# Seven block products in place of eight for two feed-forward steps

## The chip, the cores and the metric

The kernel runs on one core of one Trainium2 chip. The metric is the device time of one launch in microseconds (us), lower is better. Every time below is from that core.

## The reference

Two layers, each of a feed-forward block, a mixer of three attention branches, and a second feed-forward block, over 256 tokens with 1024 features. The change touches the feed-forward blocks alone; there are four in the run:

```python
D_MODEL = 1024
SEQ = 256
DEPTH = 2
D_FF = 2816

def _swiglu(x, w_gate, w_up, w_down):
    return (jax.nn.silu(x @ w_gate) * (x @ w_up)) @ w_down
...
    for l in range(DEPTH):
        x = x + 0.5 * _swiglu(_rmsnorm(x, ffn1_norm[l]), ffn1_w_gate[l], ffn1_w_up[l], ffn1_w_down[l])
...
        x = x + 0.5 * _swiglu(_rmsnorm(x, ffn2_norm[l]), ffn2_w_gate[l], ffn2_w_up[l], ffn2_w_down[l])
    return _rmsnorm(x, final_norm)
```

## The kernel before

**Three passes.** Every float32 operand is split in two float32r parts, a rounded one (`_hi`) and the rest (`_lo`), and every product is three matmuls: hi by hi, hi by the weights' lo, lo by the weights' hi (`three`, lines 1393 to 1395). The normalised and turned input stands in `ht_hi`, `ht_lo` (1024 features in 8 blocks `k` of 128 rows, 256 tokens in 2 tiles `t` of 128).

**The ring of slabs.** Weights come as slabs of 128 x 2048 float32 (1 MB) through a ring of three slots: `raw`, `whi`, `wlo`. SP loads a slab with two DMAs of 512 KB as soon as its slot's `raw` has been read (it waits for `lo_done` of the slab three before); ScalarE rounds it into `whi` (`convert`, L1138); VectorE subtracts and writes the rest into `wlo` (`convert`, L547); both wait until TensorE has used the slab three before (`slab_used`).

**A step.** A feed-forward block runs in 11 steps (`NSTEP`) of 256 hidden columns (`FSTEP`). Step i has two slabs of gate and up weights (4 blocks k each, 256 gate columns beside 256 up columns) and one slab of down weights. `gate_up(i)` is 2 slabs x 4 blocks x 2 tiles x 3 passes = 48 matmuls of 512 columns into PSUM banks 0 and 1 (tile t in bank t); `down(i)` is 24 matmuls into banks 4 to 7, which gather the block's output over all steps. TensorE's order is gate_up(i), down(i-1), gate_up(i+1), down(i), so the product of step i has one down and one gate_up in which to get ready.

**Between them.** After gate_up(i), ScalarE computes silu of the gate half into `sg` (L1178, one instruction for each tile), VectorE multiplies it with the up half and the row's scale (`products`, L599), and then turns the 256 x 256 product: 16 transposes of 32 partitions each (`turn_product`, L609), which put each 32 x 32 block at its final place. ScalarE rounds the turned product into `at_hi` (`act_round`, L1186), VectorE writes the rest into `at_lo` (`act_rest`, L615). The last two steps use other buffers and the last gate_up uses banks 2 and 3, so that TensorE runs gate_up(9), gate_up(10), down(8), down(9), down(10) at the end. After down(10) VectorE adds the result to `x` (`residual`, L588) and the next block's input is turned by TensorE (`prep`, L1412), rounded by ScalarE, and the rest written by VectorE (L571).

**What sets the order.** Each engine's program is written out by hand in a block of its own, and runs in order; all synchronisation is by counted semaphores. GpSimd (POOL) has nothing to do in a feed-forward block but the row scales; in the mixer it issues DMAs that move 32 x 32 blocks between partitions (`cross`, L1103), the method that the change brings to the feed-forward steps.

## Time and profile before

| | |
|---|---|
| median of 3 runs | 1160.47 us (1158.66 to 1160.72) |
| profiled execution | 1159.99 us, its span 1158.2 us |
| TensorE busy | 1148.3 us, 99% of the span, 5525 matmuls |
| VectorE busy | 935.0 us, 81% |
| ScalarE busy | 581.5 us, 50% |
| GpSimd busy | 73.5 us, 6% |
| DMA | 186 GB/s mean |
| granted TensorE clock | 0.998 |

The span is the time from the first to the last instruction of the profiled execution; the device time has a little more around it. A busy share near 100% on one engine says that it sets the time as long as nothing makes it wait.

### The profile page before, as it was taken

Reading aid. Unit: us, or ns where it says so; the run is one execution under the profiler, and the core shown is the slowest. Engines: PE = TensorE matmul, PEld = TensorE weight load, DVE = VectorE, ACT = ScalarE, POOL = GpSimd, SP = SyncE. Lnnn points to the kernel's source line nnn. Section 1 sums busy time; section 2 is a strip of 40 time slices with the busy share of each in tenths; the row PEclk is TensorE's granted clock in tenths of the full one; section 3 lists DMA queues with packets and bytes.
Section 4 is the critical chain, followed back from the end, with each engine's and each line's share of the span. In section 5 each row is a group of like instructions: output and inputs, shape, how many; then the busy total and the mean of one; then the engine's idle time right before and its main releaser. Section 6 shows DMA issues by size and latency. Waiting matters only on the chain.

```text
span 1158.2 us, 16246 instructions
## 1 busy us (share of the span) xinstructions
PE 1148.3 (99%) x5525; PEld 940.3 (81%) x5525; DVE 935.0 (81%) x1734; ACT 581.5 (50%) x757; POOL 73.5 (6%) x133
## 2 busy tenths in 40 slices
PE   9999999999999999999999999999999999999997
PEld 6888888887777888888888888888877788888886
DVE  6877887878977688778887887877898696888877
ACT  6444345456764464344454444454678635434433
POOL 2000000061000000000000000002510000000000
PEclk9999999999999999999999999999999999999999
DMA  8566555796325555655556556557943345655570
GB/s 289 189 214 216 179 187 163 238 252 199 135 74 182 182 161 202 217 192 183 195 177 202 180 178 218 182 183 216 281 155 108 144 142 182 219 181 168 197 236 37
DMA packets 151042, 215.21 MB, mean 186 GB/s; under 512 B 9184, under 2 KB 110160, under 8 KB 150992
## 3 DMA queue, kind: packets, MB, share of 16 engines
q1 hardware_dynamic: 148256, 209.64, 55.2%
q0 software_dynamic: 2048, 4.20, 1.6%
q10 hardware_dynamic: 688, 0.71, 0.2%
q8 instruction: 30, 0.49, 0.2%
q14 instruction: 20, 0.16, 0.0%
HBM read 209.28 MB, written 1.05 MB: 182 GB/s over the span
## 4 chain that ended last, share of the span: by engine, by line
PE 96%; DMA 2%; DVE 1%; issue 0%; SPq 0%; ACT 0%; POOLq 0%; POOL 0%; DVEq 0%
PE ps L1393 30%; PE ps L1395 29%; PE ps L1394 29%; PE ps L1607 2%; PE ps L1663 1%; PE ps L1635 1%; PE ps L1443 1%; DMA raw<-in_w_in_dram 1%; PE ps L1412 1%; DMA x<-in_x_dram 1%; DVE wlo L547 0%; PE ps L1694 0%; PE ps L1654 0%; SPq L508 0%; PE ps L1578 0%
## 5 line engine op out<-in xcount | busy, mean ns | idle before, releaser
L547 DVE TENSOR_TENSOR wlo<-raw,whi 128x2048 fp32r<-128x2048 f32 (+1 forms) x195 | 433.7, 2242 | 79.8 <-ACT whi L1138 57.7
L1138 ACT ACTIVATE whi<-raw 128x2048 fp32r<-128x2048 f32 (+1 forms) x195 | 366.1, 1879 | 257.6 <-PE ps L1395 251.7
L1393 PE MATMUL ps<-whi,ht_hi 128*128 128x512 f32 (+1 forms) x1192 | 465.5, 391 | 0.6 <-DVE wlo L547 0.6
L1395 PE MATMUL ps<-whi,ht_lo 128*128 128x512 f32 (+1 forms) x1192 | 460.8, 387 | 0.0
L1394 PE MATMUL ps<-wlo,ht_hi 128*128 128x512 f32 (+1 forms) x1192 | 460.3, 386 | 0.0
L1395 PEld LDWEIGHTS ps<-whi,ht_lo 128*128 128x128 f32 x1192 | 223.9, 188 | 46.0
L1393 PEld LDWEIGHTS ps<-whi,ht_hi 128*128 128x128 f32 x1192 | 224.0, 188 | 45.6 <-ACT whi L1138 1.1
L1394 PEld LDWEIGHTS ps<-wlo,ht_hi 128*128 128x128 f32 x1192 | 224.1, 188 | 43.7
L609 DVE STREAM_TRANSPOSE scr<-scr 32x128 f32<-32x128 f32 x688 | 208.4, 303 | 10.3
L1393 PE MATMUL ps<-whi,at_hi 128*128 128x512 f32 x304 | 118.5, 390 | 0.0
L1394 PE MATMUL ps<-wlo,at_hi 128*128 128x512 f32 x304 | 118.3, 389 | 0.0
L1395 PE MATMUL ps<-whi,at_lo 128*128 128x512 f32 x304 | 118.3, 389 | 0.0
L1178 ACT ACTIVATE scr<-ps,rstd 128x256 f32<-128x256 f32 x88 | 37.0, 472 | 130.2 <-PE ps L1395 129.7
L599 DVE SCALAR_TENSOR_TENSOR scr<-ps,rstd,scr 128x256 f32<-128x256 f32 x88 | 38.5, 479 | 55.8 <-ACT scr L1178 55.8
L1393 PEld LDWEIGHTS ps<-whi,at_hi 128*128 128x128 f32 x304 | 57.0, 188 | 12.5 <-issue 0.8
L1395 PEld LDWEIGHTS ps<-whi,at_lo 128*128 128x128 f32 x304 | 57.1, 188 | 11.9
L1394 PEld LDWEIGHTS ps<-wlo,at_hi 128*128 128x128 f32 x304 | 57.1, 188 | 11.8
L1272 ACT ACTIVATE prob<-prob,nmax 128x128 f32<-128x128 f32 (+1 forms) x96 | 42.4, 447 | 6.3 <-DVE nmax L768 6.1
L1089 POOL TENSOR_SCALAR msq<-ssq 128x2 f32<-128x2 f32 x6 | 1.2, 193 | 656.6 <-ACT p_t L1151 656.6
L1166 ACT ACTIVATE ht_hi<-ps,cols 128x256 fp32r<-128x256 f32 x47 | 19.2, 473 | 29.8 <-PE ps L1412 29.8
L1117 POOL TENSOR_SCALAR gates<-gates 128x512 f32<-128x512 f32 x24 | 21.7, 920 | 173.8 <-ACT gates L1244 173.8
L1237 ACT ACTIVATE proj<-ps,rstd 128x512 f32<-128x512 f32 (+1 forms) x24 | 14.2, 644 | 32.9 <-PE ps L1395 32.9
(179 smaller groups left out, 787.4 us busy)
## 6 DMA issues: line engine op xcount, KB each, us to landing
raw<-in_ffn_w_down_dram SPq DMA_DIRECT2D x88, 512.0 KB, 4.8
raw<-in_w_in_dram SPq DMA_DIRECT2D x88, 512.0 KB, 4.6
raw<-in_ffn_w_gate_dram SPq DMA_DIRECT2D x85, 512.0 KB, 4.0
raw<-in_ffn_w_up_dram SPq DMA_DIRECT2D x85, 512.0 KB, 5.0
raw<-in_w_out_dram SPq DMA_DIRECT2D x16, 512.0 KB, 4.5
raw<-in_w_branch_c_dram SPq DMA_DIRECT2D x8, 512.0 KB, 4.2
qk<-gates POOLq DMA_DIRECT2D x32, 64.0 KB, 2.9
gates<-prob POOLq DMA_DIRECT2D x32, 64.0 KB, 6.3
```

The costliest lines, as they stand in the source:

```text
L547: nc.vector.tensor_tensor(wlo[:, n, 0:w], raw[:, n, 0:w], whi[:, n, 0:w].bitcast(F32), ALU.subtract).then_inc(lo_done, 1)
L599: nc.vector.scalar_tensor_tensor(act[:, t, :], ps[:, bank, FSTEP:2 * FSTEP], rstd[:, t:t + 1], sg[:, t, :], ALU.mult, ALU.mult).then_inc(a ...
L609: ins = nc.vector.transpose(dst[q:q + 32, :, :, a:a + 32], src[a:a + 32, :, :, q:q + 32])
L1117: nc.gpsimd.tensor_scalar(gv, gv, 0.5, 0.5, ALU.mult, ALU.add).then_inc(gate_ready, 1)
L1138: nc.scalar.activation(whi[:, n, 0:w], raw[:, n, 0:w], ACT.Copy).then_inc(hi_done, 1)
L1166: nc.scalar.activation(ht_hi[:, k, :], src, ACT.Copy, scale=gain(l, n, k)).then_inc(hth, 1)
L1178: nc.scalar.activation(sg[:, t, :], ps[:, t + step_bank(f, i), 0:FSTEP], ACT.Silu, scale=rstd[:, t:t + 1]).then_inc(silu_done, 1)
L1272: ins = nc.scalar.activation(pv, pv, ACT.Exp, scale=-1.0, bias=nmax[:, b, 4 * t + h:4 * t + h + 1], accum_out=den[:, b, 4 * t + h:4 * t + ...
L1393: nc.tensor.matmul(o, xh, wh, start=start, stop=False)
L1394: nc.tensor.matmul(o, xh, wl, start=False, stop=False)
L1395: return nc.tensor.matmul(o, xl, wh, start=False, stop=stop)
L1607: ins = nc.tensor.matmul(score_head(t, h), queries(row, qb + h // 2, t), keys(row, pair, kb, h // 2, t + 1), start=opens, stop=n >= 6, ski ...
```

## The change

**Seven products for eight.** Steps 8 and 9 (`PAIR` = 8 and the one after) become one (`gate_up_pair`). Their gate and up weights are four blocks of 512 rows x 512 columns, B11 (gate, rows 0 to 511), B12 (up, same rows), B21 and B22 (rows 512 to 1023); the input gives four blocks of 128 tokens x 512 features. Eight block products of 12 matmuls become seven by Strassen's scheme (in Winograd's form), whose inputs are blocks and sums of blocks and whose outputs are added up afterwards.

**Sums of the weights.** The four blocks are loaded once more, whole, into `sum_raw` (8 DMAs of 512 KB spread over steps 2 to 5, `load_part`); VectorE forms four differences (`block_sum`, steps 4 to 6), ScalarE rounds them (`sum_round`, steps 5 to 7), VectorE writes the rests (`sum_rest`, steps 6, 7 and in the pair). B11 (as two half slabs), B21 and B22 also come through the ring.

**Sums of the input** (the standing side of the matmuls): ten additions of 128 x 512 (`side_sums`, five each in steps 1 and 2), four roundings and four rests in step 3.

**Outputs.** The first product is copied from its bank by ScalarE, so is the second; the others are added onto banks by the matmuls themselves or by VectorE (`pair_sums`, `pair_products`). Silu and products of the pair are on 128 x 512.

**Turning by blocks and DMA.** In all steps but the first, VectorE turns the product with 2 transposes of 128 partitions, which leave each 32 x 32 block turned in its own partitions; 16 DMAs of 16 KB, 11 issued by GpSimd and 5 by ScalarE (`cross_act`), move the blocks to their places in `act_blocks` (or, for the last two products, in `T3`'s raw buffer), and `act_round` waits for them. The step loops of VectorE, ScalarE and SP are written out; silu waits for `act_done` and no longer for `atl`.

```diff
+        m1_out = scr[:, 0:512]
+        m5_out, u2, v57, up_1 = (sum_raw["T1"][:, 512 * n:512 * n + 512] for n in range(4))
+        up_0, gate_1 = v57, m5_out
+        sg_2, act_2 = (gated_all[:, 1024 * n:1024 * n + 1024].rearrange("p (t c) -> p t c", t=NT) for n in range(2))
+
+        act_turns = [(v[:, 0:512], v[:, 512:1024]) for v in
+                     (act_blocks, sum_raw["T3"][:, 0:1024], sum_raw["T3"][:, 1024:2048])]
...
+        BY_ACT = [(3, 0), (3, 1), (3, 2), (3, 3), (2, 3)]
+        BY_POOL = [(a, q) for a in range(4) for q in range(4) if (a, q) not in BY_ACT]
...
+        def cross_act(eng, l, f, i, blocks, done):
+
+            eng.wait_ge(act_turned, (l * 2 + f) * NSTEP + i)
+            apart(eng)
+            for a, q in blocks:
+                blocks_in, blocks_out = act_set(i)
+                eng.dma_start(blocks_out[32 * q:32 * q + 32, P * a:P * a + P],
+                              blocks_in[32 * a:32 * a + 32, P * q:P * q + P]).then_inc(done[n_set(i)], 16)
...
-                for a in range(0, P, 32):
-                    for q in range(0, P, 32):
-                        ins = nc.vector.transpose(dst[q:q + 32, :, :, a:a + 32], src[a:a + 32, :, :, q:q + 32])
...
+                    for t in range(NT):
+                        ins = nc.vector.transpose(dst[:, t], src[:, t, :].rearrange("p (j q c) -> p q j c", j=2, q=4))
...
+                o, a, b, parts = ((b11, b12, b11, (0, 1)), (b12, b22, b12, (2,)), (b22, b22, b11, ()),
+                                  (b21, b21, b22, (3,)))[m]
...
+            def pair_sums(l, f):
+
+                r = l * 2 + f
+                dve.wait_ge(pair_out, r * 2 + 2)
+                dve.wait_ge(pair_ps, r * 4 + 2)
+                nc.vector.tensor_tensor(v57, ps[:, 0, :], m5_out, ALU.add).then_inc(pair_sum, 1)
+                dve.wait_ge(pair_ps, r * 4 + 3)
+                nc.vector.tensor_tensor(u2, ps[:, 3, :], m1_out, ALU.add).then_inc(pair_sum, 1)
+                dve.wait_ge(pair_sum, r * 5 + 2)
+                nc.vector.tensor_tensor(up_1, v57, u2, ALU.add).then_inc(pair_sum, 1)
+
+            def pair_products(l, f):
+
+                r, s0 = l * 2 + f, f * (FFN_SLABS + MIX_SLABS)
+                dve.wait_ge(pair_sum, r * 5 + 3)
+                wait_used(dve, l, s0 + PAIR_SLAB + 3)
+                nc.vector.tensor_tensor(up_0, ps[:, 2, :], u2, ALU.add).then_inc(pair_sum, 1)
+                dve.wait_ge(pair_sum, r * 5 + 4)
+                dve.wait_ge(silu_done, r * (2 * NSTEP) + PAIR * 2 + 2)
+                nc.vector.scalar_tensor_tensor(act_2[:, 0, :], up_0, rstd[:, 0:1], sg_2[:, 0, :], ALU.mult,
+                                               ALU.mult).then_inc(act_done, 2)
+                dve.wait_ge(pair_ps, r * 4 + 4)
+                nc.vector.tensor_tensor(gate_1, ps[:, 0, :], u2, ALU.add).then_inc(pair_sum, 1)
+                dve.wait_ge(silu_done, r * (2 * NSTEP) + PAIR * 2 + 4)
+                nc.vector.scalar_tensor_tensor(act_2[:, 1, :], up_1, rstd[:, 1:2], sg_2[:, 1, :], ALU.mult,
+                                               ALU.mult).then_inc(act_done, 2)
...
-                with dve.Fori(1, last - 1) as i:
-                    convert(l, (i, s0 + 2))
+                for i in range(1, PAIR):
+                    w = SLAB // 2 if i == PAIR - 1 else SLAB
+                    convert(l, s0 + 3 * i + 2, w)
                     products(l, f, i)
                     turn_product(l, f, i)
-                    convert(l, (i, s0 + 3))
-                    convert(l, (i, s0 + 4))
-                    act_rest(l, f, i)
-                convert(l, s0 + 3 * last - 1)
-                products(l, f, last - 1)
-                turn_product(l, f, last - 1)
-                convert(l, s0 + 3 * last)
-                act_rest(l, f, last - 1)
-                convert(l, s0 + 3 * last + 1)
+                    convert(l, s0 + 3 * i + 3, w)
+                    if i < PAIR - 1:
+                        convert(l, s0 + 3 * i + 4)
+                    if i < 3:
+                        side_sums(l, f, i - 1)
+                    if i == 3:
+                        for m in range(4):
+                            side_rest(l, f, m)
+                    for m in {4: (0,), 5: (1, 2), 6: (3,)}.get(i, ()):
+                        block_sum(l, f, m)
+                    for m in {6: (0,), 7: (1, 2)}.get(i, ()):
+                        sum_rest(l, f, m)
+                    if i < PAIR - 1:
+                        act_rest(l, f, i)
+                for m in range(2, 5):
+                    convert(l, s0 + PAIR_SLAB + m)
+                act_rest(l, f, PAIR - 1)
+                pair_sums(l, f)
+                sum_rest(l, f, 3)
+                convert(l, s0 + PAIR_SLAB + 5)
+                pair_products(l, f)
+                turn_product(l, f, PAIR)
+                turn_product(l, f, PAIR + 1)
+                convert(l, s0 + OUT_SLAB)
+                convert(l, s0 + OUT_SLAB + 1)
                 products(l, f, last)
                 turn_product(l, f, last)
-                convert(l, s0 + 3 * last + 2)
+                act_rest(l, f, PAIR)
+                convert(l, s0 + OUT_SLAB + 2)
+                act_rest(l, f, PAIR + 1)
+                convert(l, s0 + OUT_SLAB + 3)
                 act_rest(l, f, last)
                 if not ends(l, f):
-                    convert(l, s0 + 3 * last + 3)
+                    convert(l, s0 + FFN_SLABS)
...
+            def ffn(l, f):
+                norm(l * 3 + 2 * f)
+                with pool.Fori(1, PAIR) as i:
+                    cross_act(pool, l, f, i, BY_POOL, act_crossed_rest)
+                for i in range(PAIR, NSTEP):
+                    cross_act(pool, l, f, i, BY_POOL, act_crossed_rest)
+
...
-                        eng.wait_ge(atl, r * NSTEP + i)
+                        eng.wait_ge(act_done, r * (2 * NSTEP) + i * 2)
...
-                with eng.Fori(1, last - 1) as i:
-                    convert(l, (i, s0 + 2))
+                for i in range(1, PAIR):
+                    w = SLAB // 2 if i == PAIR - 1 else SLAB
+                    convert(l, s0 + 3 * i + 2, w)
                     silu(l, f, i, False)
-                    convert(l, (i, s0 + 3))
-                    convert(l, (i, s0 + 4))
-                    act_round(l, f, i)
-                convert(l, s0 + 3 * last - 1)
-                silu(l, f, last - 1, False)
-                convert(l, s0 + 3 * last)
-                act_round(l, f, last - 1)
-                convert(l, s0 + 3 * last + 1)
+                    convert(l, s0 + 3 * i + 3, w)
+                    cross_act(eng, l, f, i, BY_ACT, act_crossed)
+                    if i < PAIR - 1:
+                        convert(l, s0 + 3 * i + 4)
+                    if i == 3:
+                        side_round(l, f)
+                    for m in {5: (0,), 6: (1, 2), 7: (3,)}.get(i, ()):
+                        sum_round(l, f, m)
+                    if i < PAIR - 1:
+                        act_round(l, f, i)
+                convert(l, s0 + PAIR_SLAB + 2)
+                wait_used(eng, l, s0 + PAIR_SLAB + 1)
+                nc.scalar.activation(m1_out, ps[:, 1, :], ACT.Copy).then_inc(pair_out, 1)
+                convert(l, s0 + PAIR_SLAB + 3)
+                eng.wait_ge(pair_ps, (l * 2 + f) * 4 + 1)
+                nc.scalar.activation(m5_out, ps[:, 2, :], ACT.Copy).then_inc(pair_out, 1)
+                convert(l, s0 + PAIR_SLAB + 4)
+                act_round(l, f, PAIR - 1)
+                convert(l, s0 + PAIR_SLAB + 5)
+                wait_used(eng, l, s0 + PAIR_SLAB + 2)
+                pair_silu(l, f, 0, ps[:, 1, :])
+                convert(l, s0 + OUT_SLAB)
+                eng.wait_ge(pair_sum, (l * 2 + f) * 5 + 5)
+                pair_silu(l, f, 1, gate_1)
+                cross_act(eng, l, f, PAIR, BY_ACT, act_crossed)
+                convert(l, s0 + OUT_SLAB + 1)
+                cross_act(eng, l, f, PAIR + 1, BY_ACT, act_crossed)
                 silu(l, f, last, False)
-                convert(l, s0 + 3 * last + 2)
+                act_round(l, f, PAIR)
+                convert(l, s0 + OUT_SLAB + 2)
+                cross_act(eng, l, f, last, BY_ACT, act_crossed)
+                act_round(l, f, PAIR + 1)
+                convert(l, s0 + OUT_SLAB + 3)
...
+                pe.wait_ge(act_done, r * (2 * NSTEP) + PAIR * 2)
+                for h in range(2):
+                    product(1, quadrant(halves, 0, 0), from_ring(s0 + PAIR_SLAB + h, 2), True, 2 * h)\
+                        .then_inc(slab_used, 1)
+                pe.wait_ge(side_l, r * 4 + 4)
+                product(2, s1, from_sums("T1"), True).then_inc(pair_ps, 1)
+                product(0, s3, from_sums("T3"), True).then_inc(pair_ps, 1)
+                product(3, s2, from_sums("T2"), True).then_inc(pair_ps, 1)
+                pe.wait_ge(pair_out, r * 2 + 2)
+                product(1, quadrant(halves, 0, 1), from_ring(s0 + PAIR_SLAB + 2, 4), False).then_inc(slab_used, 1)
+                product(2, s4, from_ring(s0 + PAIR_SLAB + 3, 4), False).then_inc(slab_used, 1)
+                pe.wait_ge(pair_sum, r * 5 + 1)
+                product(0, quadrant(halves, 1, 1), from_sums("T4"), False).then_inc(pair_ps, 1)
...
-                with pe.Fori(2, last - 1) as i:
+                with pe.Fori(2, PAIR) as i:
                     gate_up(l, f, i)
                     down(l, f, i - 1, (i, s0 + 1))
-                gate_up(l, f, last - 1)
+                gate_up_pair(l, f)
                 gate_up(l, f, last)
-                down(l, f, last - 2, s0 + 3 * last)
-                down(l, f, last - 1, s0 + 3 * last + 1)
+                for n in range(3):
+                    down(l, f, PAIR - 1 + n, s0 + OUT_SLAB + n)
...
+                for i in range(i0, PAIR):
+                    if i == 2:
+                        sp.wait_ge(x_new, (l * 3 + 2 * f) * 4 + 4)
+                        sp.wait_ge(ssq_done, (l * 3 + 2 * f) * NT + NT)
                     for a in range(2):
-                        load_gate_up(l, (i, s0 - 1 + a), wg, wu, a, i * FSTEP)
-                    load_halves(l, (i, s0 + 1), wd, i * FSTEP - FSTEP, 2, 0, D)
-                for i in (last - 1, last):
-                    for a in range(2):
-                        load_gate_up(l, gate_slab(f, i) - 1 + a, wg, wu, a, i * FSTEP)
-                for i in (last - 2, last - 1):
-                    load_halves(l, s0 + 2 * last + 2 + i, wd, i * FSTEP, 2, 0, D)
+                        load_gate_up(l, s0 + 3 * i - 1 + a, wg, wu, a, i * FSTEP)
+                        if i >= 2 and a:
+                            load_part()
+                    load_halves(l, s0 + 3 * i + 1, wd, i * FSTEP - FSTEP, 2, 0, D)
+                    if i >= 2:
+                        load_part()
+                assert not parts
```

What stands in GpSimd's program between the two row-scale groups at the start of a layer; before, nothing (the three rows of each):

```order
L1089 TENSOR_SCALAR msq<-ssq 128x2 [waits x_in2,x_in0,x_in1,ssq_done]
L1091 TENSOR_TENSOR rstd<-msq,mhalf 128x2 [waits rstd_ready]
L1094 TENSOR_SCALAR hrstd<-rstd 128x2 [waits rstd_ready]
L1089 TENSOR_SCALAR msq<-ssq 128x2 [waits ssq_done]
L1091 TENSOR_TENSOR rstd<-msq,mhalf 128x2 [waits rstd_ready]
L1094 TENSOR_SCALAR hrstd<-rstd 128x2 [waits rstd_ready]
```

and now, where `act_blocks` holds the turned product and the loop of the middle rows runs over steps 1 to 7:

```order
L1283 TENSOR_SCALAR hrstd<-rstd 128x2 [waits rstd_ready]
L1296 UNCONDITIONAL_BRANCH
L534 DMA act_blocks<-act_blocks 32x128 [waits act_turned]
L534 DMA act_blocks<-act_blocks 32x128 x10
L1296 REGISTER_ALU
L1296 COMPARE_AND_BRANCH
L534 DMA act_blocks<-act_blocks 32x128 [waits act_turned]
L534 DMA act_blocks<-act_blocks 32x128 x10
L534 DMA T_raw<-T_raw 32x128 [waits act_turned]
```

Eleven DMA issues for each of ten steps have come between the two groups, each wave behind a wait for that step's transposes.

VectorE at the end of a block before, from step 9's products on (`wlo` is a slab's rest, `ht_lo` the last product's, `x` the residual; the transposes are L609):

```order
L599 SCALAR_TENSOR_TENSOR scr<-ps,rstd,scr 128x256 [waits silu_done] x2
L609 STREAM_TRANSPOSE scr<-scr 32x2x2x32 [waits act_done]
L609 STREAM_TRANSPOSE scr<-scr 32x2x2x32 x15
L547 TENSOR_TENSOR wlo<-raw,whi 128x2048 [waits slab_used,hi_done,raw_in2]
L615 TENSOR_TENSOR ht_lo<-scr,ht_hi 128x512 [waits ath]
L547 TENSOR_TENSOR wlo<-raw,whi 128x2048 [waits slab_used,hi_done,raw_in0]
L588 SCALAR_TENSOR_TENSOR x<-ps,x 128x512 [waits sub_out] x2
```

and now, the pair, from the third slab of it on (`T_lo` is the rest of a weight sum, `T_raw<-ps` the sums of banks):

```order
L637 TENSOR_TENSOR wlo<-raw,whi 128x2048 [waits slab_used,hi_done,raw_in2]
L637 TENSOR_TENSOR wlo<-raw,whi 128x2048 [waits slab_used,hi_done,raw_in0]
L713 TENSOR_TENSOR at_lo<-act_blocks,at_hi 128x512 [waits ath]
L764 TENSOR_TENSOR T_raw<-ps,T_raw 128x512 [waits pair_ps,pair_out]
L766 TENSOR_TENSOR T_raw<-ps,scr 128x512 [waits pair_ps]
L768 TENSOR_TENSOR T_raw<-T_raw 128x512 [waits pair_sum]
L756 TENSOR_TENSOR T_lo<-T_raw,T_hi 128x2048 [waits sum_h]
L637 TENSOR_TENSOR wlo<-raw,whi 128x2048 [waits slab_used,hi_done,raw_in1]
L775 TENSOR_TENSOR T_raw<-ps,T_raw 128x512 [waits slab_used,pair_sum]
L778 SCALAR_TENSOR_TENSOR gated_T<-T_raw,rstd,gated_T 128x512 [waits silu_done,pair_sum]
L781 TENSOR_TENSOR T_raw<-ps,T_raw 128x512 [waits pair_ps]
L783 SCALAR_TENSOR_TENSOR gated_T<-T_raw,rstd,gated_T 128x512 [waits silu_done]
```

Between the rests of slabs stand now the output sums, each behind a product of TensorE, and one rest of a weight sum.

## Rows read from the trace of the kernel before

**Rows 1.** The page's head and busy time, share of span and count by engine.

```profile
span 1158.2 us, 16246 instructions
...
PE 1148.3 (99%) x5525; PEld 940.3 (81%) x5525; DVE 935.0 (81%) x1734; ACT 581.5 (50%) x757; POOL 73.5 (6%) x133
```

**Rows 2.** Waits of TensorE: total us, times, longest.

```profile
PE ps L1786 <- DVE scr L986: 1.3, 1, 1.3
...
PE ps L1393 <- DVE wlo L547: 0.6, 2, 0.3
```

**Rows 3.** Timeline of TensorE, step's first down and next gate_up matmul: start, us, work.

```profile
128.32 0.39 PE L1393 MATMUL ps<-whi,at_hi 128*128 128x512 f32 x1
...
133.76 0.39 PE L1393 MATMUL ps<-whi,ht_hi 128*128 128x512 f32 x1
```

**Rows 4.** Timeline of VectorE through that step.

```profile
129.03 0.88 DVE L599 SCALAR_TENSOR_TENSOR scr<-ps,rstd,scr 128x256 f32<-128x256 f32 x2 [1.71 <-ACT scr L1178]
129.95 5.05 DVE L609 STREAM_TRANSPOSE scr<-scr 32x128 f32<-32x128 f32 x16
135.03 4.49 DVE L547 TENSOR_TENSOR wlo<-raw,whi 128x2048 fp32r<-128x2048 f32 x2
139.44 0.69 DVE L615 TENSOR_TENSOR at_lo<-scr,at_hi 128x512 fp32r<-128x512 f32 x1
141.35 2.29 DVE L547 TENSOR_TENSOR wlo<-raw,whi 128x2048 fp32r<-128x2048 f32 x1 [1.23 <-ACT whi L1138]
```

**Rows 5.** Timeline of ScalarE through that step.

```profile
128.53 0.84 ACT L1178 ACTIVATE scr<-ps,rstd 128x256 f32<-128x256 f32 x2 [3.52 <-PE ps L1395]
129.26 1.91 ACT L1138 ACTIVATE whi<-raw 128x2048 fp32r<-128x2048 f32 x1
133.97 1.92 ACT L1138 ACTIVATE whi<-raw 128x2048 fp32r<-128x2048 f32 x1 [2.79 <-PE ps L1395]
135.79 0.61 ACT L1186 ACTIVATE at_hi<-scr 128x512 fp32r<-128x512 f32 x1
139.41 1.92 ACT L1138 ACTIVATE whi<-raw 128x2048 fp32r<-128x2048 f32 x1 [3.00 <-PE ps L1395]
```

**Rows 6.** Groups by line and shape: busy us, mean ns, idle before.

```profile
L558 DVE TENSOR_TENSOR wlo<-raw,whi 128x1024 fp32r<-128x1024 f32 x3 | 3.6, 1223 | 1.8 <-ACT whi L1146 1.8
...
L707 DVE STREAM_TRANSPOSE prob<-gates 128x256 f32<-128x256 f32 x8 | 3.0, 414 | 0.0
```

**Rows 7.** Timeline of GpSimd in the mixer, and one ScalarE DMA issue.

```profile
231.26 9.42 POOL L1103 DMA_DIRECT2D qk<-gates  x16 [33.46 <-DVE gates L707]
245.43 0.97 POOL L1110 MEMSET gates<- 128x1024 f32 x1 [4.75 <-DMA qk<-gates]
...
0.81 0.46 ACTq L1130 DMA_DIRECT2D rows<-in_rows_dram  x1
```

**Rows 8.** Landing of GpSimd's DMAs issued at 231.3 and at 239.9 to 240.8.

```profile
DMA to landing us min/median/max: 3.1/3.1/3.1
...
DMA to landing us min/median/max: 4.9/5.1/5.3
```

**Rows 9.** Windows, feed-forward steps and mixer: busy, clock, DMA share, GB/s.

```profile
26.00:153.00 127.00, 127.00 (x562) 105.16 (x561) 102.58 (x176) 55.98 (x48) 0.00 (x0) 1.00 0.60 198
220.00:240.00 20.00, 20.00 (x90) 16.53 (x89) 15.87 (x17) 7.57 (x8) 8.74 (x15) 1.00 0.86 235
```

**Rows 10.** End of the first block: timelines of VectorE, then TensorE.

```profile
184.29 0.69 DVE L588 SCALAR_TENSOR_TENSOR x<-ps,x 128x512 f32<-128x512 f32 x1 [0.52 <-PE ps L1395]
185.65 0.69 DVE L588 SCALAR_TENSOR_TENSOR x<-ps,x 128x512 f32<-128x512 f32 x1 [0.67 <-PE ps L1395]
...
188.45 0.87 DVE L571 SCALAR_TENSOR_TENSOR ht_lo<-ps,cols,ht_hi 128x256 fp32r<-128x256 f32 x2
...
186.81 0.60 PE L1412 MATMUL ps<-ident,x 128*128 128x128 f32 x4
...
189.08 0.47 PE L1393 MATMUL ps<-whi,ht_hi 128*128 128x512 f32 x1
```

More of the change, by code:

```diff
@@ L1490, in gate_up @@
                 r, s0 = l * 2 + f, f * (FFN_SLABS + MIX_SLABS)
-                if not first and not final(i):
+                if final(i):
+                    pe.wait_ge(pair_sum, r * 5 + 4)
+                elif not first:
                     pe.wait_ge(act_done, r * (2 * NSTEP) + i * 2)
```

181 lines of the change are left out of this document (163 added, 18 removed).

## Prediction

> **What bounds the kernel now.** I read the page's head first: TensorE is busy for 99% of the 1158.2 us span, VectorE 81%, ScalarE 50%, GpSimd 6% [rows 1]. The waits of TensorE confirm that nothing holds it up: its longest is 1.3 us at the start, and VectorE's slab rests cost it 0.6 us in the whole run [rows 2]. So the time is the number of matmuls times their spacing, and it changes by what is taken from TensorE and by new waits of TensorE. The spacing is read from its timeline: the 24 matmuls of a down begin at 128.32 and the next gate_up at 133.76, so 5.44 / 24 = 0.2267 us each (the 0.39 us of a row is a pipelined length). A step of 72 is then 16.32 us, gate_up 10.88 us [rows 3]. I write T for the moment at which gate_up(i) gives way to down(i-1), here 128.32.
>
> **What is removed.** In each block 96 matmuls of steps 8 and 9 become 84. All are 512 columns wide with a standing side of 128 x 128, as before, so four blocks lose 48 x 0.2267 = 10.9 us. The granted clock is 1.00 through the steps [rows 9] and no gap is removed that could have lowered it. This is the whole gain: VectorE's shorter turning is worth nothing by itself, since VectorE isn't waited for.
>
> **A normal step after the change.** Silu begins at T+0.2 [rows 5], the products run from T+0.7 to T+1.6 [rows 4]. The 16 transposes (5.05 us) become two of 128 x 256 at 0.41 us [rows 6]: they end at T+2.4 where the old ones ended at T+6.7. Then comes what is new, the crossing. GpSimd issues 11 DMAs. Its only issues in the trace are the mixer's, 9.42 / 16 = 0.589 us each [rows 7]; those carry 64 KB in 256-byte runs, the new ones 16 KB in 512-byte runs, so I take 0.589 as the upper bound; the lower is zero, and nothing would be gained below it but the passage at the end of the block. The eleventh is issued at T+2.5+5.9 = T+8.4. From issue to landing the trace has 3.1 us where the DMA engines were little loaded, and 4.9 to 5.3 under the mixer's burst [rows 8]. The steps have a DMA share of 0.60 at 198 GB/s against 0.86 at 235 in the stretch of those issues [rows 9], so I take the near end, 3.1: all landed at T+11.5. ScalarE's own five issues at 0.46 us [rows 7] start when the second slab is rounded, T+2.9, and end at T+5.2, before its next rounding at T+5.65 [rows 5]; they cost nothing. Rounding (0.61) and rest (0.69) put `at_lo` at T+12.9, or T+15.1 with 5.3 us of landing. TensorE wants it at T+16.3. No wait either way, taken alone.
>
> **The loop that could be too long.** ScalarE rounds the next slab behind the product's rounding (before at T+11.1, 139.41 [rows 5]), VectorE needs that for its rest, and the next products stand behind the rest. From the last issue on: landing 3.1, rounding 0.61, slab rounding 1.92, slab rest 2.25, products 0.88, transposes 0.8, hops 0.3; with ten issues of 0.589 this is 15.8 us against the step's 16.3. It fits by 0.5 us, so the crossing doesn't set the pace. The margin is thin, and it is the first rival.
>
> **The sums' load on VectorE.** An addition of 128 x 512 is 0.69 us (`act_rest` [rows 4]), of 128 x 2048 2.25. Per step come 5 x 0.7 = 3.5 us (steps 1, 2), 2.8 (step 3), 2.25 (step 4), 4.5 (steps 5 and 6). Both slab rests of a step now end at T+9.8 (the second behind its rounding from T+5.65 to T+7.6), so the worst step reaches T+14.3, its `act_rest` T+15.0: 1.3 us before TensorE asks. VectorE is saved 4.2 us per step by the turning. ScalarE has 3.8 us more at most. The extra 4 MB per block come in steps 2 to 5, 1 MB to a step of 3 MB: by proportion 198 x 4/3 = 264 GB/s and a share of 0.80. Cost: nothing.
>
> **The pair.** Let T be the end of gate_up(7). Down(6) ends at T+5.4, then products of 2.72 us: first to T+8.2, then T1 10.9, T3 13.6, T2 16.3, B21 19.0, B22 21.8, T4 24.5, then gate_up(10). ScalarE, in order: half slab 2.0, five issues 4.8, rounding of T4 6.7, slab 8.6, copy of bank 1 9.2, slab 11.1, copy of bank 2 11.7, slab 13.6, product 14.2. VectorE: half slab (1.22 [rows 6]) to T+4.1, rests of T3 and T2 to 8.6, slabs to 10.9, 13.4 and 15.9, `act_rest` 16.5, three sums to 18.7, rest of T4 to T+21.0, wanted at 21.8. Then a slab rest to T+23.4 and `up_0` to T+24.1, wanted by gate_up(10) at 24.5, since it frees bank 2. Each fits, by 0.8 and 0.4 us. Cost 0; up to 1 us per block if my hops are short.
>
> **The end of the block.** The pair's two products are ready at T+27, turned at 27.8 and 28.6; GpSimd has 22 issues from T+27.9 to T+40.9, then eleven for the last product to 47.4; landed at T+49.9, rounded 50.5, rest 51.2. Down(10) starts at T+51.7, so this holds by 0.5 us. But a slab rounding and rest stand behind it, to T+54.7, and then the residual. Before, that slab's rest had ended 0.5 us before the residual could start [rows 10]; now the first residual, possible at T+53.2, starts 1.5 us late, the second ends at 56.0 where TensorE's turning wants it at 55.8. Before, the rest of the new input began at 188.45 (one of the two instructions done at 188.9) and its matmul ran at 189.08 [rows 10], with 0.2 us to spare. So some 0.8 us are lost at the passage into the next block, if an issue takes the full 0.589. Three blocks have such a passage, 2.4 us in all; with issues of 0.55 or less it is nothing (33 x 0.04 = 1.3 us earlier). Between 0 and 2.4 I take 1.5, nearer the bound that has a row.
>
> **The sum.** Against the profiled execution, 1159.99 us (span 1158.2 and 1.8 around it): 1160.0 - 10.9 + 1.5 = 1150.6. The median of the runs is 0.5 us above it: 1151.1.
>
> **Pages of the Trainium skill that bear on it.** "DMA: Bandwidth & Descriptors", Anatomy of one DMA, gives a small DMA a fixed cost of about 2 us, nearly all completion; an estimate by that page lands the crossing a microsecond sooner than 3.1 us and makes the passage free, 1149.6 us. "SBUF — State Buffer", Who interferes with whom and the box on SWDGE, speaks against the change: a DMA issued from GpSimd that takes 620 ns alone takes some 3100 ns beside VectorE's two-port copies, because GpSimd can't write descriptors then. By that figure eleven issues would be 34 us, twice a step. The same page limits it to copies, casts and tensor_scalar in SBUF, of which these steps have none, and the issues in rows 7 kept 0.589 us beside a VectorE busy 15.87 of 20 us [rows 9].
>
> **Rivals.**
> (a) The crossing sets the pace (slower). Place: GpSimd's eleven issues and their landing, in steps 1 to 7. For it: the loop's margin of 0.5 us, and the 5.3 us landings of rows 8, which came with heavier DMA traffic, and the T loads bring some. Against: a quarter of the bytes, larger runs. At 5.3 us the loop is 18.0, 1.7 over, for six steps 10 us, less the 1.2 us by which `at_lo` was early, so 9 per block; the end of the block adds 2.2. Times four 45, less 10.9: about 1194 us. It decides (time above before) from a landing of about 4.3 us on, or issues above 0.7.
> (b) VectorE late in the pair. If its chain through three sums, a weight rest, a slab rest and `up_0` is 1.5 us longer than I have it, TensorE waits about 1.1 us per block: 1155.5 us. At 3.1 us of lateness per block the gain is gone.
> (c) The change doesn't bring what it says: the twelve matmuls are gone, but pair and end of the block together wait 2.7 us per block. For it: both margins are under a microsecond, and the lateness adds up. Time 1160, no change.
> (d) GpSimd's issues are held up by VectorE, as a mechanism of this kernel: its two-input additions or transposes slow each issue from 0.589 us to, say, 0.8. The loop is then 17.9 and the time as in (a), near 1195. Rows 7 speak against it.
>
> **How the numbers follow.** Forecast, gain of 10.9 less small waits at the passages (1148.5 to 1154): 0.68. (b), 1154 to 1158: 0.10. (c): 0.07. (a) at all strengths: 0.12. (d): 0.03. The range from 1148.5 to 1159 takes in the forecast, (b) and some of (c), a little over 0.8; the forecast's own range is 1148.5 to 1154. This kernel's measurement tells about 0.2% (2.3 us) from no change. Faster by more: forecast and (b), 0.78. Within: (c), 0.07. Slower: (a) and (d), 0.15.
>
> **What would show each step.** Right: 5525 matmuls less 48; TensorE's waits under 5 us; `act_round` beginning near T+11.5; GpSimd's eleven issues 6.5 us; VectorE busy well below 81%; the rest of T4 at T+21, `up_0` at T+24. Wrong: a wait of TensorE on `atl` growing from step to step (a), on `pair_sum` or `sum_l` (b), at L588 or L571's successors (the passage).

## The result: 1170.6 us, slower by 0.9%

The changed kernel takes 1170.63 us (median of 4 runs, 1168.66 to 1172.07), the kernel before 1160.58 beside it: ratio 1.0092, interval 1.0079 to 1.0104. The forecast of 1151.1 and its range up to 1159 were both missed: the time rose where a fall was forecast. The profiled execution of after took 1170.92 us.

The page's head and busy time of after, which answer to [rows 1]:

```profile
span 1169.2 us, 15632 instructions
...
PE 1144.6 (98%) x5477; PEld 933.1 (80%) x5477; DVE 881.7 (75%) x1274; ACT 612.7 (52%) x789; POOL 289.0 (25%) x573
```

The 48 matmuls are gone (5525 to 5477), VectorE has less to do, and the span is 11.0 us longer. The waits of TensorE, which answer to [rows 2]:

```profile
PE ps L1630 <- DVE at_lo L713: 5.2, 10, 1.1
PE ps L2007 <- ACT gates L1481: 3.9, 2, 3.5
PE ps L2067 <- DVE scr L1175: 1.3, 1, 1.3
```

This list names the places but not the whole loss; the time between the starts of successive downs gives that. In before every single step takes 16.32 us. In after, block 2 has 16.50, 16.89, 16.90, 16.46, 17.55 and 16.44, then 35.46 for the stretch with the pair, which without a wait would take 35.36 (all in us). So the difference can be laid out:

| Where | us |
|---|---|
| matmuls of the pair | -10.9 |
| single steps, four blocks (2.0, 2.8, 2.4, 1.9) | +9.0 |
| pair stretches (0.3) and the last down's start in block 4 (0.7) | +1.1 |
| mixer of layer 1 (first turning of its input to that of the next block: 209.0 before, 215.2 after) | +6.2 |
| from the last matmul's start to the end (7.2 before, 13.4 after) | +6.2 |
| rest (mixer of layer 0, passages between blocks) | -0.6 |
| difference of the spans | +11.0 |

**The single steps.** Timeline of ScalarE in after, two steps of block 2 (`[...]` is the idle time before a row and what ended it):

```profile
452.12 0.64 ACT L1384 ACTIVATE at_hi<-act_blocks 128x512 fp32r<-128x512 f32 x1 [5.25 <-DMA act_blocks<-act_blocks]
452.66 1.90 ACT L1334 ACTIVATE whi<-raw 128x2048 fp32r<-128x2048 f32 x1
...
458.63 3.09 ACTq L534 DMA_DIRECT2D act_blocks<-act_blocks  x5
...
469.02 0.63 ACT L1384 ACTIVATE at_hi<-act_blocks 128x512 fp32r<-128x512 f32 x1 [3.20 <-issue]
```

VectorE's timeline between:

```profile
454.64 2.29 DVE L637 TENSOR_TENSOR wlo<-raw,whi 128x2048 fp32r<-128x2048 f32 x1 [1.17 <-ACT whi L1334]
456.85 0.87 DVE L689 SCALAR_TENSOR_TENSOR scr<-ps,rstd,scr 128x256 f32<-128x256 f32 x2
457.76 0.77 DVE L707 STREAM_TRANSPOSE act_blocks<-scr 128x256 f32<-128x256 f32 x2
```

And GpSimd's:

```profile
459.12 5.39 POOL L534 DMA_DIRECT2D act_blocks<-act_blocks  x11 [11.49 <-DVE act_blocks L707]
```

This is the loop of rival (a), closed. It goes from the rounding of a product at 452.12 through slab rounding, slab rest, products and turning to the first issue at 459.12 (7.0 us), and from there in 9.9 us to the next rounding at 469.02: 16.9 us, the very length of that step. Eleven issues take 4.9 us from first to last start, so 5.0 us remain from the last issue to the rounding; the last of the sixteen landed at 468.94, so it is the landing that ended the wait for which the row says "issue". The window of block 1's steps, which answers to the first of [rows 9], shows what the transfers meet there: a DMA share of 0.75 where it had been 0.60.

```profile
26.00:153.00 127.00, 125.91 (x553) 103.21 (x552) 96.55 (x86) 64.28 (x57) 37.98 (x77) 1.00 0.75 246
```

In step 5 something else ends last. ScalarE, then VectorE, in that step of block 2, whose T is 487.1:

```profile
491.75 3.10 ACTq L534 DMA_DIRECT2D act_blocks<-act_blocks  x5
494.95 1.92 ACT L1334 ACTIVATE whi<-raw 128x2048 fp32r<-128x2048 f32 x1 [4.75 <-issue]
```
```profile
499.17 4.61 DVE L750 TENSOR_TENSOR T_raw<-T_raw 128x2048 f32<-128x2048 f32 x2
503.70 0.69 DVE L713 TENSOR_TENSOR at_lo<-act_blocks,at_hi 128x512 fp32r<-128x512 f32 x1
```

The product had been rounded at 501.9, but VectorE was still at the two sums of weight blocks, and `at_lo` came when they were done. The late loop had pushed them back: ScalarE's five issues ended at T+7.8, its slab rounding began at T+7.9 instead of T+5.65, and the sums ended at T+16.7. It is so in all four blocks (the rounding is done 1.8 to 2.2 us before `at_lo` starts), and step 5 alone is 3.5 of the 9.0 us.

**The second mixer.** Timeline of GpSimd:

```profile
802.48 4.14 POOL L1292 DMA_DIRECT2D qk<-gates  x7 [33.41 <-DVE gates L896]
808.21 5.18 POOL L1292 DMA_DIRECT2D qk<-gates  x9 [1.60 <-issue]
820.02 0.96 POOL L1306 MEMSET gates<- 128x1024 f32 x1 [6.63 <-DMA qk<-gates]
```

In the first mixer of before the sixteen issues run without a gap and the memset waits 4.75 us [rows 7]; here 1.60 us are missing behind the seventh, and the memset waits 6.63 (4.09 in the second mixer of before). What queues behind it is SP (SyncE), which loads a table only when these transfers have landed, and the weight slabs only then. Timelines of SP, ScalarE and TensorE:

```profile
819.99 0.37 SPq L2186 DMA_DIRECT2D gates<-in_cmp_w_k_dram  x1
820.40 15.65 SPq L2089 DMA_DIRECT2D raw<-in_w_in_dram  x8
```
```profile
837.43 1.91 ACT L1334 ACTIVATE whi<-raw 128x2048 fp32r<-128x2048 f32 x1 [5.50 <-DMA raw<-in_w_in_dram]
```
```profile
840.77 0.66 PE L2007 MATMUL ps<-fold,p_t 128*128 128x64 f32 x2 [3.48 <-ACT gates L1481]
841.19 0.77 PE L1630 MATMUL ps<-whi,ht_hi 128*128 128x512 f32 x1
841.76 0.63 PE L1631 MATMUL ps<-wlo,ht_hi 128*128 128x512 f32 x1
842.19 0.63 PE L1632 MATMUL ps<-whi,ht_lo 128*128 128x512 f32 x1
```

TensorE stands for 3.48 us, and then its matmuls come 0.43 us apart: the window 838 to 847 has a granted clock of 0.62, that is partly at 1.2 GHz. A wait of TensorE cost its own length and the slow matmuls behind it.

**The end.** One line of the program (the closing barrier) in after:

```profile
L142 POOLq DRAIN  x1: 10981/10981/10981, 1158.0 to 1158.0; - x1
```

GpSimd's own closing instruction lasts 10.98 us, and all engines wait for it, though SP had seen the output landed at 1162.1. The same in before:

```profile
L135 POOLq DRAIN  x1: 1995/1995/1995, 1153.2 to 1153.2; - x1
```

### The profile page after: what moved, and what is told of

It is laid out like the page before. It is cut to its first block and busy times, and to the rows that moved or that the text cites. A ratio compares the mean times of both kernels' runs of the same rounds, so it can differ in the third digit from the quotient of the medians.

```text
span 1169.2 us, 15632 instructions
## 1 busy us (share of the span) xinstructions
PE 1144.6 (98%) x5477; PEld 933.1 (80%) x5477; DVE 881.7 (75%) x1274; ACT 612.7 (52%) x789; POOL 289.0 (25%) x573
## 5 line engine op out<-in xcount | busy, mean ns | idle before, releaser
L637 DVE TENSOR_TENSOR wlo<-raw,whi 128x2048 fp32r<-128x2048 f32 (+2 forms) x195 | 426.7, 2193 | 169.2 <-ACT whi L1334 148.7
L1334 ACT ACTIVATE whi<-raw 128x2048 fp32r<-128x2048 f32 (+2 forms) x195 | 358.6, 1841 | 224.8 <-issue 115.7
L1630 PE MATMUL ps<-whi,ht_hi 128*128 128x512 f32 (+1 forms) x1064 | 416.7, 392 | 0.6 <-DVE wlo L637 0.3
L1632 PE MATMUL ps<-whi,ht_lo 128*128 128x512 f32 (+1 forms) x1064 | 411.9, 387 | 0.0
L1631 PE MATMUL ps<-wlo,ht_hi 128*128 128x512 f32 (+1 forms) x1064 | 411.5, 387 | 0.0
L534 POOL DMA_DIRECT2D act_blocks<-act_blocks x352 | 173.1, 500 | 412.1 <-DVE act_blocks L707 409.8
L1632 PEld LDWEIGHTS ps<-whi,ht_lo 128*128 128x128 f32 x1064 | 200.4, 188 | 41.1
L1631 PEld LDWEIGHTS ps<-wlo,ht_hi 128*128 128x128 f32 x1064 | 200.7, 189 | 38.8
L534 POOL DMA_DIRECT2D T_raw<-T_raw x88 | 43.1, 498 | 0.2 <-issue 0.2
L1396 ACT ACTIVATE T_hi<-T_raw 128x2048 fp32r<-128x2048 f32 x16 | 30.1, 1906 | 14.8 <-issue 14.8
```

What stands on the lines that cost most here:

```text
L534: eng.dma_start(blocks_out[32 * q:32 * q + 32, P * a:P * a + P], blocks_in[32 * a:32 * a + 32, P * q:P * q + P]).then_inc(done[n_set(i)], 16)
L637: nc.vector.tensor_tensor(wlo[:, n, 0:w], raw[:, n, 0:w], whi[:, n, 0:w].bitcast(F32), ALU.subtract).then_inc(lo_done, 1)
L1334: nc.scalar.activation(whi[:, n, 0:w], raw[:, n, 0:w], ACT.Copy).then_inc(hi_done, 1)
L1396: nc.scalar.activation(sum_hi[SUMS[m]][:, :], sum_raw[SUMS[m]][:, :], ACT.Copy).then_inc(sum_h, 1)
L1630: nc.tensor.matmul(o, xh, wh, start=start, stop=False)
L1631: nc.tensor.matmul(o, xh, wl, start=False, stop=False)
```

## The experiments

All are timed beside the kernel before (1159.9 to 1160.2 us in these sets); runs 8 and 12 were timed only once. "Period" is the time from the start of one down to the next.

**1. What the transfers cost when nobody waits for them.** The kernel before, with eleven more issues at each turning (`act_turned`), into a buffer that the feed-forward doesn't use:

```diff
+                for i in range(1, NSTEP):
+                    pool.wait_ge(act_turned, (l * 2 + f) * NSTEP + i)
...
+                        pool.dma_start(spare[32 * q:32 * q + 32, P * a:P * a + P],
+                                       ident[32 * a:32 * a + 32, :]).then_inc(spare_in, 16)
```

> The kernel before, with 11 block transfers per step (10 steps, 4 blocks: 440 in all) issued by GpSimd from the identity matrix into a buffer that the feed-forward does not use; nothing waits for them inside a block. Theory (what 440 GpSimd transfers cost although nobody waits for them): GpSimd's closing drain grows from 2.0 us to about 11 us, so the end comes 6 to 7 us later than in the kernel before, and the mixer of layer 1 may lose some us to a pause in GpSimd's issuing; the single steps stay at 16.3 us. Time 1167 to 1173. Rival (the drain and the pause belong to the transfers' being waited for, or to the changed kernel's traffic): drain near 2 us, time 1160 to 1162.

Measured: 1166.6 us (1.0057, 1.0040 to 1.0074). Periods 16.31 to 16.33; mixer of layer 1 209.0; three pauses in GpSimd's issuing (from one start to the next 2.4 us at its 129th transfer, 6.8 at the 271st, 2.8 at the 399th), none where it held anything up; closing drain 10.98 us. So the 6.4 us over before are the drain's (from the last matmul's start to the end 13.4 us against 7.2): the transfers held nothing up where nothing waited for them.

**2 and 3. Without the crossing.** The 16 transposes again in steps 1 to 7 (`DIRECT` is 0 to 7), then in 1 to 4 and 7 (0 to 4 and 7):

```diff
         def direct(i):
-            return isinstance(i, int) and i == 0
+            return i in DIRECT
```

> The changed kernel with the turned product of single steps 1 to 7 made by the 16 transposes on VectorE as before, without crossing transfers; only the pair's two and the last step's still cross (33 GpSimd transfers a block, 132 and the mixer's 64). Theory (the crossing's length sets the pace of the single steps): steps 1 to 4 and 7 return to 16.3 us; in steps 5 and 6 VectorE has 13.2 us of step work and 4.5 us of sums, 17.7 us against 16.3, so up to 1.4 us each may be lost there; drain near 2 + 132 x 0.02 = 4.6 us. 1160.5 - 10.9 + 2.6 (drain) + 0 to 11 (VectorE in steps 5 and 6) = 1152 to 1163, likeliest 1156. Rival (VectorE's sums, not the crossing, lengthen the steps): steps 1 to 7 as long as in the changed kernel or longer, 16.5 to 18 us each, over 1170.

> As the run before, but steps 5 and 6, where VectorE subtracts three and rounds one of the weight sums, keep the crossing; 55 GpSimd transfers a block. Theory (crossing sets the pace where it is used, VectorE where it is not): steps 1 to 4 and 7 at 16.3 us, steps 5 and 6 lose up to 0.7 us each; drain near 2 + 220 x 0.02 = 6.4 us against 2.0. 1160.5 - 10.9 + 4.4 + 0 to 5 = 1154 to 1159, likeliest 1157. Rival (VectorE's sums lengthen the steps): over 1168.

Measured: 1168.8 us (1.0074) and 1164.38 us (1.0035, 1.0021 to 1.0049). Both are above what I expected (1152 to 1163 and 1154 to 1159). Steps 1 to 4 are back at 16.32 (at most 16.49), so it was the crossing, and not the sums, that had lengthened them. Steps 5 and 6 take 16.55 and 17.6 when direct, and 16.32 each when crossing behind four direct steps, as in run 3: on their own neither their crossing nor their sums make them late. I had missed one thing: both runs lose in the pair's stretch, 37.6 us against 35.4. Waits of TensorE in run 2:

```profile
PE ps L1765 <- DVE wlo L640: 4.3, 4, 1.1
PE ps L1633 <- DVE at_lo L716: 4.0, 4, 1.0
PE ps L1765 <- DVE T_lo L759: 2.1, 4, 0.5
```

With 4.3 us more on VectorE in step 7, the pair's slab rest and `T_lo` are late, 2.2 us in every block (the third row is the rest of a sum). The crossing is needed there.

**4. A drain where it is hidden.** `pool.drain()` behind the last wave, 16 us before GpSimd's last instruction.

> The changed kernel with one drain of GpSimd more, right behind its last wave of crossing transfers, some 25 us before its last work. Theory (the closing drain of GpSimd clears up after the transfers it issued, about 20 ns each, and nothing hides it since it starts with GpSimd's last work): the early drain takes about 9 us or more and is hidden, the closing one is back near 2 us or less, and the time falls by 6 to 7 us from the changed kernel's, to about 1164. Rival (a drain costs what it costs each time it is made, by the count of all transfers so far): both take 11 us, and the time stays at 1170 to 1171.

Measured: 1163.28 us (1.0028), 7.3 below the changed kernel. The early drain and the closing one:

```profile
L1316 POOLq DRAIN  x1: 11512/11512/11512, 1141.3 to 1141.3; - x1
...
L142 POOLq DRAIN  x1: 662/662/662, 1157.8 to 1157.8; - x1
```

The closing drain's length hangs on what was issued since the last one, and an early drain under other work costs nothing.

**5. The best version.** Transposes in steps 1 to 4, crossing in 5, 6, 7 and the last three; drains at each block's start and behind the last wave.

> The changed kernel with the 16 transposes in single steps 1 to 4 only (crossing in 5, 6, 7 and the last three), and drains of GpSimd at the start of each block and behind its last wave. Theory: the run with step 7 direct too measured 1164.4 and lost 2.1 us a block in the pair by VectorE's late roundings (pair stretch 37.56 against 35.45 us) and 9.6 us in the closing drain; with step 7 crossing again the stretch returns to 35.5 (8 us less over four blocks), and the closing drain falls to 0.7 us (8.9 less, of which up to 7 was exposed): 1164.4 - 8 - 7 = 1148 to 1151. Rival (the crossing of step 7 meets a full ScalarE and costs as in the changed kernel, or the drains at block starts hold up GpSimd's norm work or first wave): 1153 or more.

Measured: 1149.95 us (0.9914, 0.9900 to 0.9928), 20.7 below the changed kernel and 10.2 below before. Periods 16.32 (steps 2 and 3 of the later blocks 16.4 to 16.7), pair stretch 35.36, mixer 209.2, no pause over 0.9 us. The page and TensorE's waits:

```profile
span 1147.9 us, 15485 instructions
...
PE 1138.6 (99%) x5477; PEld 931.3 (81%) x5477; DVE 945.7 (82%) x1498; ACT 614.8 (54%) x789; POOL 202.9 (18%) x397
```
```profile
PE ps L2072 <- DVE scr L1178: 1.3, 1, 1.3
PE ps L1635 <- DVE bt_lo L716: 0.7, 1, 0.7
```

**6. Drains alone,** at the block starts and behind the last wave of the changed kernel.

> The changed kernel with GpSimd drained at the start of each block (behind the block's norm work, before its first wave) and behind the last wave; all else as changed. Theory (the pauses of about 2 us in GpSimd's issuing come when some count of transfers since it last cleared up is reached, and the one in the second mixer costs 6 us there): no pause over 1.5 us is left in the mixer's waves, the stretch from the first block's end to the third's... of layer 1's mixer returns from 215 to 209 us, and with the closing drain short the time is 1163.3 (the run with one early drain) - 6 = 1157 to 1159. Rival (the pauses do not depend on drains): pauses at the same transfers, 1163 or more.

Measured: 1158.92 us (0.9990, 0.9981 to 1.0000), 11.7 below the changed kernel. Mixer of layer 1: 213.0, not 209. One pause was left there, at the 129th transfer since the last drain (1.86 us at 820.0); the one that had come with the 271st was gone. The time came out as expected, the mixer only by a third; periods stay long.

**7. Without the extra loads.** In blocks 2 to 4 the parts for the sums aren't loaded:

```diff
-                parts = [(n, h) for n in range(4) for h in range(2)]
+                parts = [(n, h) for n in range(4) for h in range(2)] if r == 0 else []
...
+                if r:
+                    a = b = x[:, :, :].rearrange("p t c -> p (t c)")
```

> The changed kernel in which blocks 2 to 4 do not load the four weight parts for the sums (4.2 MB a block less in steps 2 to 5) and VectorE subtracts residual rows instead, so the result of these blocks' pair is not the reference's; crossing as changed. Theory A (the crossing transfers land late because they share the 16 DMA engines with the extra loads): in blocks 2 to 4 the product's rounding starts 8 to 9 us after the wave's first issue in all steps, and the single steps of blocks 2 to 4 lose under 0.7 us a block instead of 2.4 to 2.9; time 1164 to 1165. Theory B (ScalarE's five issues of 0.63 us and its wait for the turned product push its roundings back, whatever the traffic): losses stay at 2 to 3 us a block, time 1169 to 1171.

VectorE subtracts rows of `x` in their place, so its work is the same. Measured: 1162.47 us (1.0016), 1.5 below the theory's range. Blocks 2 to 4: all periods 16.32; block 1, which still loads: 16.33, 16.97, 16.45, 17.13, 16.44, much as in the changed kernel. That is theory A: with the loads gone the same loop, the same sums and the same issues of ScalarE fit. The other way in which loads could act, slabs that arrive late, isn't it: the trace of block 2 of the changed kernel shows no wait of ScalarE or VectorE for a slab's load. From the wave's first issue to the rounding in steps 1 to 3 of block 2 it is 9.6, 8.8 and 8.9 us, in the changed kernel 11.4, 9.9 and 9.9. ScalarE's timeline here:

```profile
449.00 0.63 ACT L1386 ACTIVATE at_hi<-act_blocks 128x512 fp32r<-128x512 f32 x1 [4.17 <-DMA act_blocks<-act_blocks]
449.54 1.90 ACT L1336 ACTIVATE whi<-raw 128x2048 fp32r<-128x2048 f32 x1
452.87 0.84 ACT L1376 ACTIVATE scr<-ps,rstd 128x256 f32<-128x256 f32 x2 [1.43 <-PE ps L1634]
```

Its silu now waits for TensorE, the sign that TensorE leads. The median landing barely shows it (share of the DMA engines 0.65 against 0.73); groups of GpSimd's issues, 420 to 550 us of after and 417 to 545 of this run (KB each, median us to landing):

```profile
act_blocks<-act_blocks POOLq DMA_DIRECT2D x78, 16.0 KB, 4.1
```
```profile
act_blocks<-act_blocks POOLq DMA_DIRECT2D x77, 16.0 KB, 3.8
```

A wave is done with its slowest of sixteen, so what counts is the 5.0 us from last issue to rounding against 3.9, not 4.1 against 3.8.

**8. Whose transfers the closing drain is for.** Run 1 with the waves in layer 0 only; timed once.

> The kernel before with the 11 spare GpSimd transfers a step in layer 0's two blocks alone: 284 GpSimd transfers in all, none but the second mixer's 32 in the last 560 us. Theory (the closing drain grows with the count of transfers of the whole run): about 9.6 us, as in the run of the changed kernel with 284. Rival (it clears up what was issued lately): about 2 us, as in the kernel before.

Measured: 1160.95 us, closing drain 3.30 us. It is neither theory nor rival: 284 transfers in all gave 9.59 us in run 3 and 3.30 here. The other closing drains: 64 transfers 2.0, 196 (run 2) 6.9, 328 (run 11) 10.5, 504 (after, run 1) 11.0, but 704 (run 12) 3.3; directly behind a drain 0.7. The pauses seem to clear up too: run 12 issued 31 transfers behind its last pause and run 8 13, against 101 in run 11 and over 100 in after and run 1. So I read it as growing with what was issued since the last drain or pause, up to about 11 us; but the 29 of run 2 gave 6.9, and I have no rule that fits all.

**9 and 10. Cutting the loop.** ScalarE's `act_round` and VectorE's `act_rest` of step i - 1 stand behind the next slab's rounding and rest; 10 has drains behind every last wave and at the start of each second feed-forward as well.

```diff
                     convert(l, s0 + 3 * i + 2, w)
+                    if i > 1:
+                        act_round(l, f, i - 1)
                     silu(l, f, i, False)
...
-                    if i < PAIR - 1:
-                        act_round(l, f, i)
```

> The changed kernel with all crossing transfers, weight parts and sums, but in single steps ScalarE rounds the product of step i - 1 (and VectorE takes its rest) behind, not ahead of, their work on the next step's first slab. Theory (the loss is a loop: rounding of a product, 7.0 us through the slab's rounding, its rest on VectorE, products and turn to the next wave's first issue, then 9.9 us to the next rounding, 16.9 against 16.3): with the slab ahead of the rounding the next wave does not depend on this one, the product's rest is ready about 14.5 us after gate-and-up against 16.3 needed, and all single steps take 16.3 us; the closing drain and the second mixer's pause stay: 1170.6 - 9 = 1161 to 1162.5. Rival (the wave alone is too long under the loads, loop or not): steps stay at 16.5 to 17.2, 1168 or more.

> As the run before, and GpSimd drained behind the last wave of every block and at the start of each layer's second feed-forward, so that it never issues more than 110 transfers between two drains. Theory: single steps 16.3 us, no pause over 1 us in GpSimd's issuing (they came at the 129th transfer since the start or a drain), layer 1's mixer back from 215 to 209 us, closing drain 0.7 us: the step saving of 10.9 us is all that is left, 1148 to 1150. Rival (drains behind the waves hold GpSimd's norm work up, or the pause comes by another count): 1152 or more.

Measured: 1171.88 us (1.0099), and 1161.28 us (1.0010, 1.0001 to 1.0019). The periods of run 9, block 2, are 17.05, 16.66, 16.46, 16.61, 17.67, 16.49: no gain. My theory expected 16.3 and fell short. The time is in the rival's range, but its reason, the wave alone too long, isn't what the trace shows. ScalarE and VectorE of run 9:

```profile
57.97 1.92 ACT L1334 ACTIVATE whi<-raw 128x2048 fp32r<-128x2048 f32 x1 [3.52 <-PE ps L1632]
59.80 0.61 ACT L1384 ACTIVATE at_hi<-act_blocks 128x512 fp32r<-128x512 f32 x1
```
```profile
60.26 2.28 DVE L637 TENSOR_TENSOR wlo<-raw,whi 128x2048 fp32r<-128x2048 f32 x1
62.47 0.69 DVE L713 TENSOR_TENSOR at_lo<-act_blocks,at_hi 128x512 fp32r<-128x512 f32 x1
...
106.21 4.61 DVE L750 TENSOR_TENSOR T_raw<-T_raw 128x2048 f32<-128x2048 f32 x2
110.74 2.29 DVE L637 TENSOR_TENSOR wlo<-raw,whi 128x2048 fp32r<-128x2048 f32 x1
112.94 0.69 DVE L713 TENSOR_TENSOR at_lo<-act_blocks,at_hi 128x512 fp32r<-128x512 f32 x1
```

The product's rounding no longer waits for the transfers: it starts straight behind the slab's, which itself waits for TensorE to free the slab at 57.97. From there rounding, rest and `at_lo` end at 63.2, when TensorE wants it at 63.2 to 63.4; with two block sums ahead, at 113.6, more than a microsecond late. One chain was cut, and the one put in its place is as long. Run 10 missed its 1148 to 1150, since its steps are as long as run 9's, but it shows the rest cleanly, against run 9: no pause at all, mixer 209.3 (213.6), closing drain 0.7: 10.6 us.

**11. Run 5 without its drains.**

> The run with direct turns in steps 1 to 4 (1149.95 us) without its drains; 328 GpSimd transfers in all, so a pause of about 2 us at the 129th, which falls in block 2, and another later. Theory: closing drain 7 to 10 us, 5 to 7 of it exposed, and 0 to 5 us for a pause that falls in a mixer: 1155 to 1161. Rival (the drains gave nothing): 1150 to 1151.

Measured: 1156.44 us (0.9972, 0.9961 to 0.9983). Closing drain 10.49 us, pauses in the last waves of blocks 2 and 3, outside the mixers. The drains are worth 6.5 us. The other 14.2 from the changed kernel's 1170.6 are the steps and the second mixer, where fewer transfers move the pause elsewhere.

**12. All sixteen issues on GpSimd** (`BY_ACT = []`); timed once.

> The changed kernel with all 16 transfers of a wave issued by GpSimd, none by ScalarE. Theory (loop of 7.0 us plus the wave, the wave being GpSimd's issues at 0.49 us and a landing of about 5): a wave of 16 takes 5 x 0.49 = 2.4 us more, so the loop of steps 1 to 7 goes from 16.9 to about 19 us, 2.4 us a step more: 1170 + 4 x 6 x 2.4 = 1220 to 1245. Rival (ScalarE's five issues, 3.1 us on the way of its roundings, lengthen the steps more than GpSimd's would): 1160 to 1180.

Measured: 1255.8 us. ScalarE's timeline in block 2:

```profile
461.82 0.63 ACT L1384 ACTIVATE at_hi<-act_blocks 128x512 fp32r<-128x512 f32 x1 [8.97 <-DMA act_blocks<-act_blocks]
...
481.60 0.63 ACT L1384 ACTIVATE at_hi<-act_blocks 128x512 fp32r<-128x512 f32 x1 [10.47 <-DMA act_blocks<-act_blocks]
```

The first issue of the wave is at 468.82: 7.0 us and then 12.8, 19.8 in all, the period of that step (16.9 + 5 x 0.49 = 19.3 by the loop). The total is above my 1245. The single steps of the four blocks lose 55.5 us more than in the changed kernel; the rest is at the ends of the blocks, where the waves of the last three steps, 48 issues, reach past their cover. There GpSimd also paused once in each block, for 5.1 to 5.8 us behind the first of these waves (at its 129th, 321st, 481st and 673rd transfer), longer than anywhere in the changed kernel. ScalarE's five issues were a help, not the load.

## Why the prediction was wrong

- **The matmuls: right.** 10.9 us; run 5 keeps 10.2 of them.
- **The loop that could be too long: the step that failed.** "It fits by 0.5 us, so the crossing doesn't set the pace." It was 16.9 us, not 15.8. Ten issues took 4.9 where I had 5.9 (+1.0 in my favour), the way from rounding to first issue 7.0 where I had 6.8. The landing term was mis-sized: 3.1 us from [rows 8], against 5.0 from the last issue to the rounding (3.9 in run 7, without the extra loads). I took the near end because the steps had a DMA share of 0.60 [rows 9], but with the crossing and the extra loads in the same steps it is 0.75, and the wave needs the slowest of sixteen. I had worked out 0.80 for the loads in another paragraph and held it against nothing. Rival (a) had the place right and set its threshold at a landing of 4.3 us; its weight of 0.12 was too small and its price too large, 45 us against 9 in the steps and nothing at the passages.
- **ScalarE's issues: "they cost nothing" is not shown.** I had 0.46 us each from [rows 7]; it is 0.62 here (five in 3.09). With the products late they end at T+7.8, not T+5.2, and hold back the slab rounding behind them by 2.2 us. What that costs by itself no run isolates; without the extra loads they fit (run 7), and run 12 shows only that the same five on GpSimd are dearer.
- **VectorE's sums: sized right, placed wrong.** Two take 4.6 us, forecast 4.5. But I had them end at T+14.3 in the worst step, 1.3 us in hand with `at_lo`, and they ended at T+16.7 in step 5, since the loop had made the slab rest before them late (T+12.2, not T+9.8). So in step 5 `at_lo` waits for the sums, 3.5 of the 9.0 us. Where the loop isn't late they fit: blocks 2 to 4 of run 7 have the same work and lose nothing.
- **The pair: right,** 0.1 us a block. Its margins were real, as run 2 shows.
- **The passage between blocks: 1.5 us forecast, 0 found** in the middle blocks: issues at 0.49 us were below the 0.55 that I had named as the bound.
- **Not in the sum at all:** 440 more transfers from GpSimd lengthen its closing drain by 9.0 us, 6.2 of them exposed (runs 1, 4 and 10), and bring pauses in its issuing, one of which fell into the second mixer. Without it (run 10 against run 9) that mixer was 4.3 us shorter; 6.2 us are lost there in the changed kernel. "What it adds" has to include what the new instructions leave to do on their engine.
- **GpSimd slowed by VectorE, rival (d): did not come.** The issues took 0.49 us from start to start beside a VectorE busy 75%. The Trainium skill's "SBUF — State Buffer", Who interferes with whom, ties that slowing to VectorE's copies, casts and tensor_scalar; the trace agrees in that additions and transposes didn't bring it.
- **A landing of about 2 us,** as an estimate by the Trainium skill's "DMA: Bandwidth & Descriptors", Anatomy of one DMA: the medians here were 4.1 in the changed kernel and 3.8 in run 7, so the measurement decides, and the page would have made the error larger.

What stays open: what law the drain and the pauses follow, and how much of the second mixer's 6 us is the pause itself. With other pauses there it lost 4.0 us (run 6, 1.86 us at 820.0), 1.6 (run 8, 2.4 us at 821.5) or about 0.3 (run 3, 1.86 us at 821.2).

## What to carry to other kernels

When a chain of transfers replaces an engine's work, write down the whole loop that it closes, and take for the landing the slowest of the group under the load that the change itself brings, not the median of a quieter stretch. A margin of 0.5 us out of 16 is no margin, and margins elsewhere that were worked out with the loop fitting go with it. If VectorE has slack in some steps and not in others, decide step by step who does the work. Count what an engine has to clear up at the end, and move that to where something else is running.
